# The step size columns of an input projection share the rotary keys' tile, as the first block of a layer

## The reference

```python
h = _rmsnorm(x, lp['norm1_w']) * (1 + sc1) + sh1
u = h @ lp['w_in']
u_ssd = u[..., :SSD_PROJ]
u_ret = u[..., SSD_PROJ:SSD_PROJ + RET_PROJ]
u_mla = u[..., SSD_PROJ + RET_PROJ:]
...
z = u[..., :D_SSD]
xbc = jax.nn.silu(_dwconv(u[..., D_SSD:D_SSD + CONV_DIM], conv_w, conv_b))
dt = jax.nn.softplus((u[..., D_SSD + CONV_DIM:].reshape(b, L, 2, H_SSD) + dt_bias).astype(jnp.float32))
...
ckv = _rmsnorm(u[..., Q_RANK:Q_RANK + KV_RANK], kv_norm_w)
krope = u[..., Q_RANK + KV_RANK:]
```

## Time and profile before

| what | value |
|---|---|
| device time, median of 3 runs | 1224.89 us |
| lowest and highest run | 1223.51 and 1225.37 us |
| span of the profiled execution | 1220.8 us |
| its own device time | not measured apart; the median is 4.1 us above the span |
| mean granted TensorE clock | 0.965 of full |
| TensorE busy | 1108.9 us, 91% of the span |
| VectorE, ScalarE, GpSimd busy | 584.5, 426.6, 84.9 us |
| HBM read | 156.26 MB |

### The profile page before, as it was taken

The page is one execution under the profiler, slowest core; times in us unless marked ns, Lnnn a source line. Parts: engine busy times, 40 slices in busy tenths (PEclk is TensorE's granted clock), DMA queues, the critical chain, the costliest instruction groups (busy, mean ns, idle before and its releaser), DMA issues.

```text
span 1220.8 us, 17833 instructions
## 1 busy us (share of the span) xinstructions
PE 1108.9 (91%) x6756; PEld 991.1 (81%) x6756; DVE 584.5 (48%) x949; ACT 426.6 (35%) x601; POOL 84.9 (7%) x50
## 2 busy tenths in 40 slices
PE   3598999989699999999959899989978999999996
PEld 1387987467699998999957788955868999999995
DVE  0576555665644333333346845566555344333333
ACT  3334434333433322232224433253435323322221
POOL 0213101000100000000011320020001000000000
PEclk9699999999899999999988899998998999999998
DMA  9442331602132358433344232242111333453331
GB/s 387 191 173 78 100 119 52 232 24 70 35 133 108 138 212 331 178 110 119 118 174 160 91 112 70 104 173 111 36 70 69 137 124 117 162 206 112 119 123 54
DMA packets 31359, 159.65 MB, mean 131 GB/s; under 512 B 3328, under 2 KB 4160, under 8 KB 21312
## 3 DMA queue, kind: packets, MB, share of 16 engines
q1 hardware_dynamic: 29184, 150.41, 34.1%
q10 hardware_dynamic: 2112, 8.39, 1.7%
HBM read 156.26 MB, written 2.52 MB: 130 GB/s over the span
## 4 chain that ended last, share of the span: by engine, by line
PE 78%; DVE 10%; issue 5%; ACT 4%; DMA 3%; ACTq 0%; DVEq 0%
PE ps L388 21%; PE ps L389 21%; PE ps L390 21%; DMA adas<-wada_dram 3%; PE ps L419 2%; PE ps L561 2%; PE ps L533 2%; PE ps L570 2%; PE ps L725 1%; DVE h_lo L1143 1%; ACT whi L816 1%; PE ps L707 1%; DVE v L1210 1%; ACT sq L851 1%; PE ps L645 1%
## 5 line engine op out<-in xcount | busy, mean ns | idle before, releaser
L388 PE MATMUL ps<-h_hi,whi 128*128 128x384 f32 x1184 | 410.8, 347 | 22.0 <-DVE h_lo L1143 18.6
L390 PE MATMUL ps<-h_hi,wlo 128*128 128x384 f32 x1184 | 401.8, 339 | 0.0
L389 PE MATMUL ps<-h_lo,whi 128*128 128x384 f32 x1184 | 401.8, 339 | 0.0
L388 PEld LDWEIGHTS ps<-h_hi,whi 128*128 128x128 f32 x1184 | 227.2, 192 | 35.2 <-issue 24.1
L389 PEld LDWEIGHTS ps<-h_lo,whi 128*128 128x128 f32 x1184 | 227.3, 192 | 1.3
L390 PEld LDWEIGHTS ps<-h_hi,wlo 128*128 128x128 f32 x1184 | 226.7, 191 | 0.0
L1093 DVE TENSOR_TENSOR wlo<-stage,whi 128x2048 fp32r<-128x2048 f32 (+1 forms) x68 | 154.3, 2270 | 134.4 <-ACT whi L816 75.2
L388 PE MATMUL ps<-hid_hi,whi 128*128 128x384 f32 x352 | 122.4, 348 | 0.0
L390 PE MATMUL ps<-hid_hi,wlo 128*128 128x384 f32 x352 | 118.9, 338 | 0.0
L389 PE MATMUL ps<-hid_lo,whi 128*128 128x384 f32 x352 | 118.9, 338 | 0.0
L865 ACT ACTIVATE ny<-ps 128x384 f32<-128x384 f32 x44 | 21.7, 492 | 250.8 <-PE ps L390 250.8
(11 more groups left out here) (211 smaller groups left out, 1095.7 us busy)
## 6 DMA issues: line engine op xcount, KB each, us to landing
stage<-wf_dram SPq DMA_DIRECT2D x44, 1024.0 KB, 4.9
adas<-wada_dram SPq DMA_DIRECT2D x80, 512.0 KB, 5.7
stage<-win_dram SPq DMA_DIRECT2D x22, 1024.0 KB, 4.9
stage<-wf_dram SPq DMA_DIRECT2D x32, 704.0 KB, 4.0
stage<-wout_dram SPq DMA_DIRECT2D x8, 1024.0 KB, 5.2
adaf<-wada_dram ACTq DMA_DIRECT2D x3, 2048.0 KB, 21.4
small<-small_dram SPq DMA_DIRECT2D x2, 1206.5 KB, 9.9
adas<-wada_dram ACTq DMA_DIRECT2D x1, 2048.0 KB, 34.2
```

The source lines that it names most:

```text
L388: mm(out, ah, bh, start=(k == 0), stop=False)
L389: mm(out, ah, bl, start=False, stop=False)
L390: return mm(out, al, bh, start=False, stop=(k == n - 1))
```

## The change

The 16 step size columns and the 32 rotary columns now stand in one 128-column tile: step sizes at columns 0 to 15, rotary keys at 64 to 95, zeros elsewhere. That tile is block 0, 128x1024 in all, in `first_hi`/`first_lo`. Block 8 has one tile, `ckv` alone, and is loaded, split and multiplied at half its width. The new tiles lie in bytes that the feed-forward's hidden tiles, the modulation weights and the mixers also use, so ScalarE's split of block 0 waits for the last block of the layer before and, once, for 12 used modulation blocks. ScalarE copies the rotary keys out of `ps` after block 0, and TensorE waits for this (`krope_taken`) before block 2 writes there. The permutation of the rotary keys reads 32 rows instead of 96.

```diff
 BLK = KD * 2 * P
+ONE = KD * P
...
+N_CKV = 8
...
+        krope_taken = sem("krope_taken")
...
-        dthi, dtlo = sb("dthi", [P, P], F32R), sb("dtlo", [P, P], F32R)
...
             with ExitStack() as part:
+                sb("first_gap", [P, 6 * CONVT + NCH * 512], F32, part)
+                first_hi, first_lo = (sb(n, [P, ONE], F32R, part) for n in ("first_hi", "first_lo"))
+            with ExitStack() as part:
                 v = sb("v", [P, 6, CONVT], F32, part)
...
+        def win_width(n):
+            return ONE if n == N_CKV else BLK
...
-                load_w(L, 0, 0, stage[:, 0, 0:P], wdt_d[L])
+                load_w(L, 0, 0, stage[:, 0, 0:ONE], wdt_d[L])
...
                 for n in range(2, N_WIN):
-                    load_w(L, n, n % 2, stage[:, n % 2, :], win_d[L * (N_WIN - 1) + (n - 1)])
+                    w = win_width(n)
+                    load_w(L, n, n % 2, stage[:, n % 2, 0:w], win_d[L * (N_WIN - 1) + (n - 1), :, 0:w])
...
-            def wide_block(L, n, j):
+            def wide_block(L, n, j, tiles=2):
 
                 w_ready(L, n)
-                for s in range(2):
+                for s in range(tiles):
                     for k in range(KD):
-                        last = split_mm(ps[:, 2 * j + s, 0:T], wtile(j, 2 * k + s), hk(k), k, KD)
+                        last = split_mm(ps[:, 2 * j + s, 0:T], wtile(j, tiles * k + s), hk(k), k, KD)
...
-                    last = split_mm(ps[0:16, 0, 0:T], (dthi[:, k * 16:k * 16 + 16], dtlo[:, k * 16:k * 16 + 16]),
+                    last = split_mm(ps[:, 0, 0:T], (first_hi[:, k * P:k * P + P], first_lo[:, k * P:k * P + P]),
                                     hk(k), k, KD)
...
                         pe.wait_ge(dt_taken, L + 1)
+                        pe.wait_ge(krope_taken, L + 1)
...
-                    wide_block(L, n, n % 2)
+                    wide_block(L, n, n % 2, win_width(n) // ONE)
...
-                mm(ps[hrow, 5, 0:LAT], perm, u[hrow, U_KR, CTX:T], start=True, stop=True).then_inc(krot_ps, 1)
+                krow = slice(KR0, KR0 + ROPE)
+                mm(ps[hrow, 5, 0:LAT], const[krow, K_PERM:K_PERM + NOPE + ROPE], u[krow, U_KR, CTX:T],
+                   start=True, stop=True).then_inc(krot_ps, 1)
...
-                act.wait_ge(w_used, L * NB + 1)
+                act.wait_ge(w_used, L * NB + 2)
                 act.wait_ge(stage_in[0], in_stage(L, 0))
-                f(dthi[:], stage[:, 0, 0:P], ACT.Copy).then_inc(w_hi, 1)
+                act.wait_ge(ada_used, 4 + 12)
+                f(first_hi[:], stage[:, 0, 0:ONE], ACT.Copy).then_inc(w_hi, 1)
...
                     act.wait_ge(w_used, L * NB + n + 3)
-                    if n:
+                    if n == 0:
+                        f(u[KR0:KR0 + ROPE, U_KR, :], ps[KR0:KR0 + ROPE, 0, 0:T], ACT.Copy).then_inc(krope_taken, 1)
+                    else:
...
-                        elif n == 8:
-                            f(u[:, U_CKV, :], ps[:, b, 0:T], ACT.Copy)
-                            last = f(u[:, U_KR, :], ps[:, b + 1, 0:T], ACT.Copy)
+                        elif n == N_CKV:
+                            last = f(u[:, U_CKV, :], ps[:, b, 0:T], ACT.Copy)
...
-                        split_hi(L, n + 2, n % 2)
+                        split_hi(L, n + 2, n % 2, win_width(n + 2) if n + 2 < N_WIN else BLK)
...
-                tt(dtlo[:], stage[:, 0, 0:P], dthi[:].bitcast(F32), ALU.subtract).then_inc(w_split, 1)
+                tt(first_lo[:], stage[:, 0, 0:ONE], first_hi[:].bitcast(F32), ALU.subtract).then_inc(w_split, 1)
...
                         if q < 5:
-                            split_lo(L, 8 + q, q % 2)
+                            split_lo(L, 8 + q, q % 2, win_width(8 + q) if 8 + q < N_WIN else BLK)
...
-    wdt = blocks(w_in[:, :, 1280:1296], 16).reshape(n, P, P)
+    wdt = blocks(cat([w_in[:, :, 1280:1296], np.zeros((n, D, KR0 - 16), np.float32), w_in[:, :, 2704:2736],
+                      np.zeros((n, D, P - KR0 - ROPE), np.float32)], axis=2), P).reshape(n, P, ONE)
```

More of the change, by code:

```diff
@@ L1600 @@
     cols = [w_in[:, :, s:s + 256] if s is not None else
-            cat([w_in[:, :, 2576:2704], w_in[:, :, 2640:2736], np.zeros((n, D, 32), np.float32)], axis=2)
-            for s in starts]
-    win = blocks(cat(cols, axis=2), 256).reshape(n * (N_WIN - 1), P, BLK)
-    wdt = blocks(w_in[:, :, 1280:1296], 16).reshape(n, P, P)
+            np.zeros((n, D, 256), np.float32) for s in starts]
+    win = blocks(cat(cols, axis=2), 256)
+    win[:, N_CKV - 1, :, :ONE] = blocks(w_in[:, :, 2576:2704], P)[:, 0]
+    win = win.reshape(n * (N_WIN - 1), P, BLK)
+    wdt = blocks(cat([w_in[:, :, 1280:1296], np.zeros((n, D, KR0 - 16), np.float32), w_in[:, :, 2704:2736],
+                      np.zeros((n, D, P - KR0 - ROPE), np.float32)], axis=2), P).reshape(n, P, ONE)
     wout = arr(w_out).reshape(n, 2, KW2, P, 2, 4, P).transpose(0, 1, 4, 3, 5, 2, 6).reshape(n * N_WOUT, P, BLK)
```

## The result

| | before | after |
|---|---|---|
| device time, median of 4 runs | 1225.13 us | 1239.00 us |
| lowest and highest | 1223.51 and 1231.88 us | 1237.20 and 1240.72 us |
| ratio, 95% interval | 1 | 1.0111 [1.0082, 1.0141] |
| span of the profiled execution | 1220.8 us | 1237.9 us |
| mean granted clock | 0.965 | 0.951 |

The change makes the kernel slower by 13.6 us by the ratio (10 to 17 us), where 3.8 us were forecast, and the time lies above the range. The same program's times spread by several microseconds from run to run, so I go by ratios and by places in a trace. The two profiled executions lie 17.1 us apart in span, the medians 13.9 us. The times of the kernel after lie 2.0 us above their own spans; if that holds before too, the execution profiled there was some 2 us quicker than the median.

What follows compares the result with a forecast made beforehand. TensorE's split products were taken as the bound, on 63% of the span, with VectorE's chain limiting step 2. Start 2.0, head 1.5, gain -1.2 and clock 1.5 made +3.8 on 1224.9: 1228.7 us, range 1224.4 to 1231.5.

Steps and rivals of the forecast that it cites:

- What of the fold is left: Step 2, behind block 8: 0.6 us gained per layer, 1.2 us in all; 3.5 us per layer become a wait.
- Start of the kernel: Layer 0's start: 1.1 us more load beside the modulation weights and 0.94 us more VectorE split, +2.0 us.
- Head of layer 1: Wider first-block splits, with VectorE's L1121 and GpSimd's split of block 1 colliding: +1.5 us, ends 0.75 and 1.8.
- The copy of the rotary keys: ScalarE's copy of 32 rows before `expa` fits into its idle time: cost 0, at most 0.49 us per layer.
- The clock: TensorE's new 3.5 us wait in step 2: one fall in two layers, at least 3.0 us at half speed, +1.5 us.
- rival C: The clock falls after step 2's wait in both layers: +2.3 + 3.0, 1230.2 us; chance 0.15.
- Rival E: VectorE's chain of step 2 isn't the limit, all 4.2 us of block 8 gained: -4.9, 1220.0 us; chance 0.10.
- Rival B: No fall of the clock after the new wait in step 2: +2.3, 1227.2 us; chance 0.25.
- Rival D: Cheap head: added load costs 0 at the start, layer 1 only 0.75 us: +0.5, 1225.4 us; chance 0.12.
- The constant: The three runs' median lies 4.1 us above the profiled span of 1220.8 us, and the change doesn't touch this.
- The signs: Trace marks of being right, such as step 2's 3.5 us idling and clock 0.50 in one layer, or of being wrong.
- last sign of being wrong: Falls of the clock outside step 2 change in number by more than one, which nothing in the prediction forecasts.

Runs made afterwards that it cites:

- n = 3: Kernel after the change, with 9 more matmuls behind block 8 that repeat its tile into a free bank: 1243.5 us, ratio 1.0134 [1.0085, 1.0183].

## Why the prediction was wrong

The mechanism was right, and one term of the sum was mis-sized. By its steps:

- *What of the fold is left:* 0.6 us a layer, with 3.5 us turned into a wait. Measured: L571's lag is 3.10 us in layer 0 where step 2's beginning has 3.70, so 0.6 us, and a wait of 3.56 us. Right.
- *Start of the kernel:* 1.1 us of load and 0.94 us of split. Measured in the traces 1.27 us at the first use, and 2.16 us at L1133 (44.59 for 42.43), so 0.9 us. Right, the load shown by traces alone. Its working took 427 GB/s for the whole load; the trace before has 413 to 428 GB/s from 5 to 30 us and 284 in the last 6.5 us.
- *Head of layer 1:* 1.5 us between two collisions, 1.3 or 1.7. L1135 was first, and it cost 1.1 us. Right in kind, 0.4 us high. Together the head costs 3.3 us in the traces and 3.9 us by the kernel that has it alone.
- *The copy of the rotary keys:* 0. Nothing in the lags between the head and step 2 speaks against it (0.08 and 0.42 us less); it was not tried alone.
- *The clock:* **this step failed.** "At least 3.0 us at half speed" cost 1.5 us, once. In the trace it is 5.5 us in each of the two layers: the lag grows from 3.10 to 8.61 us in layer 0, and in layer 1 by 4.87 us net of the 0.6 us gained. That is 11 us for the 1.5 assumed; put into the sum, 2.3 + 11 = 13.3 us, it gives what was measured (13.6 us, 10 to 17). Of its two parts, the number of falls (both, rival C) had a chance of 0.15. The greater error was the length. I took it from the earlier trace rows, where a dense block or a run of 128x128 transposes followed the wait, and applied it to a place where 4.6 us of L561 and L570 and 2 us of L533 stand ahead of the next dense block (at full clock, by the trace before). The transposes are narrow as well, and there the clock was back 3.4 us after they began (105.26 and 108.7 us); through L571 and L580 it stayed low for 8.3 us. Why the two differ was not tried. The work that follows was in the program, and I had read it for its order, not for its shape. The experiments bear the size out: the taking away alone costs 10.8 us, and with the wait filled 0.7 us is left of the whole loss.
- *The rivals.* Rival E, VectorE earlier: refuted, its chain kept 7.22 us. Rival B, no fall: refuted by the clock of 0.50 in both layers. Rival D, a cheap head: the traces speak against it, with a load that lands 1.27 us later and 1.1 us at layer 1; the time of the head alone, 0.7 to 7.1 us, would allow its 1.7 us. Rival C had the right count and the wrong price.
- *The constant:* the 4.1 us between median and span were called a constant. In the kernel after, each run's time is 1.9 to 2.0 us above its own span. The forecast doesn't suffer, since it was added to a median.
- *The signs:* the signs for step 2 came true, in both layers where one was forecast. The last sign of being wrong came too: outside step 2 the trace has three low stretches (64, 228 and 839 us) that the trace before hasn't. The profiled execution of the wide load alone has six such stretches, and that kernel's median is unchanged, so this sign doesn't tell the change from the spread of single executions.

A wait in front of L561 and L570 was priced from waits in front of dense matmuls and of transposes. The 3.56 us themselves were free, since the cover they replaced was as long.

What stays open: which waits make the clock fall here. 0.38 and 0.45 us did not, 2.00 us did in both layers, 2.33 us in step 1 of one layer and not of the other, so the length alone doesn't decide. Nor was it tried which of the narrow matmuls hold it low. The trace of the change speaks for L571 and L580: the clock stayed low through them in both layers and rose within L543. With n = 3 it rose about 1 us into block 9.

## What to carry to other kernels

When work is taken off TensorE, look at the engine that it is cover for: the gain is what that engine is ahead, and it pays to take the work away at the step where that is most (3.8 us in step 0, 0.65 us in step 2). Then look at what TensorE does after the new wait; here a fall of the clock cost 5.5 us a layer with L571 and L580, then L543, behind the wait. 24 useless dense ones behind the wait cut the low stretch short, but took as much time as they saved. The same number put into the wait kept the clock up and brought back 12 us; that is the time of the kernel before, not a gain over it. Only moving the narrow block was faster than before.

## What the runs showed that I had not expected

After a wait of 2.00 us the granted clock fell to 0.50 in layer 0 not in the wait but 1.6 us behind it, among the narrow matmuls, and stayed there for more than 10 us; after 3.57 us of wait it did the same in layer 1 of the kernel with the matmuls only taken away. Matmuls that compute nothing, put behind the wait, shortened the low stretch from over 12 us to about 5 us and left the time as it was (1238.73 against 1239.00 us). And executions of one program differ by up to 10 us in span: those of the wide load go from 1220.9 us at a mean granted clock of 0.966 to 1230.9 us at 0.956.
